# The forget gate's product moves to the front of the kernel, onto quarters of TensorE's columns, and the input's turnings get a third place in PSUM

## What is computed

```python
h = rmsnorm(x, norm_mix_g)
z = h @ w_in
u_pool = z[..., 0:512]; u_ssm = z[..., 512:1024]
q = z[..., 1024:1536]; k = z[..., 1536:2048]; v = z[..., 2048:2560]
logf = jax.nn.log_sigmoid(z[..., 2560:2568] + b_f)      # forget gate, 8 heads
```

## Time and profile before

| | |
|---|---|
| median of 3 runs | 1797.89 us (1792.35, 1797.89, 1801.83) |
| the profiled execution's own time | 1798.66 us |
| its span in the profile | 1796.9 us |
| TensorE (PE) busy | 1742.5 us, 97% |
| VectorE (DVE) busy | 1282.7 us, 71% |
| ScalarE (ACT) busy | 643.7 us, 36% |
| GpSimd (POOL) busy | 671.4 us, 37% |

### The profile page before, as it was taken

How to read it: one execution, slowest core, us unless ns; L and a number is a source line. 1 busy time by engine, 2 the same in 40 slices (tenths; PEclk the granted TensorE clock), 3 DMA queues, 4 the chain that set the end, 5 groups by cost and what they waited for, 6 DMA issues and landing times.

```text
span 1796.9 us, 31281 instructions
## 1 busy us (share of the span) xinstructions
PE 1742.5 (97%) x12261; PEld 1699.6 (95%) x12261; DVE 1282.7 (71%) x2006; ACT 643.7 (36%) x1239; POOL 671.4 (37%) x472
## 2 busy tenths in 40 slices
PE   7999999999998999999999988999999999999997
PEld 7999999999988989999999988999999999999997
DVE  6788662888886566554465489877777777699685
ACT  4210113566652222141002335444444444434343
POOL 4554434333354666422233223555554454000000
PEclk9999999999999999999999999999999999999999
DMA  8744838766734544365636331232222221998252
GB/s 267 220 129 137 268 108 246 194 175 176 183 111 146 129 106 94 88 191 208 196 109 207 98 108 37 74 91 89 73 73 73 73 73 55 343 345 283 93 192 90
DMA packets 265748, 267.25 MB, mean 149 GB/s; under 512 B 61985, under 2 KB 218637, under 8 KB 265154
## 3 DMA queue, kind: packets, MB, share of 16 engines
q1 hardware_dynamic: 251474, 234.04, 43.9%
q10 hardware_dynamic: 14128, 31.21, 5.0%
HBM read 181.37 MB, written 79.36 MB: 145 GB/s over the span
## 4 chain that ended last, share of the span: by engine, by line
PE 55%; DVE 6%; issue 3%; DMA 2%; ACT 1%; POOL 1%; SPq 0%; POOLq 0%; ACTq 0%; DVEq 0%
PE bank L156 51%; DMA act_raw<-act_scratch 1%; PE bank L2003 1%; PE bank L2013 1%; PE bank L2015 1%; DMA gate<-gate_scratch 1%; DVE merged L2300 1%; DVE x_forms L3087 0%; DVE prod L2293 0%; PE bank L2014 0%; DVE conv L3167 0%; DVE xt L3057 0%; POOL up_forms L2651 0%; DMA down_raw<-in_w_down 0%; PE bank L1988 0%
## 5 line engine op out<-in xcount | busy, mean ns | idle before, releaser
L156 PE MATMUL bank<-act_hi,w_hi 128*128 128x364 f32 (+1 forms) x1296 | 435.6, 336 | 2.5 <-PEq L86 1.6
L156 PE MATMUL bank<-act_lo,w_hi 128*128 128x364 f32 (+1 forms) x1296 | 427.1, 330 | 0.0
L156 PE MATMUL bank<-act_hi,w_lo 128*128 128x364 f32 (+1 forms) x1296 | 426.5, 329 | 0.0
L156 PE MATMUL bank<-x_forms,up_forms 128*128 128x272 f32 x1848 | 258.4, 289 | 3.6 <-DVE part_v L3135 2.0
L156 PEld LDWEIGHTS bank<-act_hi,w_hi 128*128 128x128 f32 x1296 | 244.9, 189 | 8.4 <-issue 4.3
L156 PEld LDWEIGHTS bank<-x_forms,up_forms 128*128 128x128 f32 x1848 | 242.2, 188 | 4.7 <-DVE up_forms L3119 2.3
L156 PEld LDWEIGHTS bank<-act_lo,w_hi 128*128 128x128 f32 x1296 | 244.8, 189 | 0.2
L156 PEld LDWEIGHTS bank<-act_hi,w_lo 128*128 128x128 f32 x1296 | 244.5, 189 | 0.0
L156 PE MATMUL bank<-act_form,down_form 128*128 128x272 f32 x1848 | 233.6, 288 | 3.6 <-DVE y_t L3243 1.8
L156 PEld LDWEIGHTS bank<-act_form,down_form 128*128 128x128 f32 x1848 | 231.7, 188 | 4.7 <-DVE y_t L3243 2.4
L2651 POOL TENSOR_TENSOR up_forms<-up_w_raw,up_forms 128x512 fp32r<-128x512 f32 x60 | 88.1, 1469 | 190.8 <-ACT up_forms L2866 190.8
(11 more groups left out here) (358 smaller groups left out, 3099.5 us busy)
## 6 DMA issues: line engine op xcount, KB each, us to landing
down_raw<-in_w_down SPq DMA_DIRECT2D x121, 256.0 KB, 4.3
w_raw<-in_w_in SPq DMA_DIRECT2D x44, 512.0 KB, 5.0
up_w_raw<-in_w_up SPq DMA_DIRECT2D x44, 512.0 KB, 4.9
gate<-gate_scratch ACTq DMA_DIRECT2D x24, 544.0 KB, 3.9
act_scratch<-ffn_act SPq DMA_DIRECT2D x22, 544.0 KB
act_raw<-act_scratch SPq DMA_DIRECT2D x44, 272.0 KB, 4.7
gate_scratch<-gate_out ACTq DMA_DIRECT2D x48, 182.0 KB, 2.7
w_raw<-in_w_out SPq DMA_DIRECT2D x14, 512.0 KB, 4.2
```

Source lines behind the costliest of these rows:

```text
L156: mm = pe.matmul(out, w(k), x(k)[:, c0:c0 + cn], start=first and k == ks[0] and n == 0, stop=last and k == ks[-1] and n == 2, skip_group_c ...
```

## The change

- The job "f" is gone from `JOBS`, and with it the split of the forget columns and DVE's six instructions that added the parts.
- `wf` is loaded by SP behind the fourth block of the input, and scaled on POOL before its second weight tile.
- Its product is taken in plain float32 from `xr`, the unrounded turned input. Each block of 128 frames is a moving operand of its own, and four blocks stand at four quarters of the array's columns (`tile_position=(0, 32 * q)`), so that their outputs lie at partitions 0, 32, 64 and 96 of one bank. `forget` is called for blocks 0 to 3 after the seventh turning, and for 4 to 7 and 8 behind the second group of q0.
- ACT copies the five pieces to a new tile `f_raw`; DVE multiplies it by `inv_b` in one instruction, right after k0 is emptied.
- The turnings have three places in PSUM instead of two; block j waits for the block that had its place before (`FREED`).
- ACT, not DVE, rounds blocks 3 and 6 into `m.hh`.
- The last bank of `acc[1]` holds the gate's sums; so q1's groups run in the order 0, 2, 1, and the third bank of `spread` is another one. A filler keeps the other tiles' addresses.

```diff
-JOBS = [("q", 0), ("q", 1), ("q", 2), ("q", 3), ("k", 0), ("f", 0), ("k", 1), ("k", 2), ("k", 3), ("v", 0), ("v", 1), ("v", 2),
+JOBS = [("q", 0), ("q", 1), ("q", 2), ("q", 3), ("k", 0), ("k", 1), ("k", 2), ("k", 3), ("v", 0), ("v", 1), ("v", 2),
-        by_k = [tr[:].rearrange("p b (k c) -> p (b k) c", c=P),
-                acc[1][:, 0:2].rearrange("p b (k c) -> p (b k) c", c=P)]
-        spread = [tr[:, 0], tr[:, 1], acc[1][:, 2]]
+        SLOT, FREED, ROUNDED = (0, 1, 2, 0, 1, 2, 0, 1, 0), (0, 0, 0, 1, 2, 3, 4, 5, 7), (3, 6)
+        by_slot = [x.rearrange("p b (k c) -> p (b k) c", c=P) for x in (tr[:], acc[1][:, 0:2], acc[0][:, 1:3])]
+        by_k = [by_slot[a] for a in SLOT]
+        spread = [tr[:, 0], tr[:, 1], acc[1][:, 1]]
+        f_bank = acc[1][:, 2]
...
+            sp.dma_start(wf[:], column_blocks(io["w_in"][0, :, 5 * W:5 * W + HEADS], KD)).then_inc(wf_ld, 16)
             for j in range(4, 9):
                 sp.wait_ge(x_turned, j - 3)
...
                 if t == 1:
+                    pool.wait_ge(wf_ld, 16)
+                    pool.tensor_tensor(wf[:], wf[:], m.gain1[:].unsqueeze(2).to_broadcast([P, KD, HEADS]), ALU.mult
+                                       ).then_inc(wf_scaled, 1)
                     pool.wait_ge(x_lo, 8)
...
-                if j >= 2:
-                    pe.wait_ge(x_lo, j - 1)
+                if j >= 3:
+                    pe.wait_ge(x_lo, FREED[j])
...
+            def forget(tokens):
+                pe.wait_ge(x_out, tokens[-1] + 1)
+                for k in range(KD):
+                    for j in tokens:
+                        (c0, cn), r0, at = TOK[j], 32 * (j % 4), j // 4 * P
+                        mm = pe.matmul(f_bank[r0:r0 + HEADS, at:at + cn], wf[:, k], xr[:, k, c0:c0 + cn], start=k == 0,
+                                       stop=k == KD - 1, tile_position=(0, r0))
+                mm.then_inc(f_mm, 1)
...
                 turn_x(5 + q)
+                if q == 1:
+                    pe.wait_ge(wf_scaled, 1)
+                    forget((0, 1, 2, 3))
             pe.wait_ge(x_lo, 6)
             group(0, 0, 1)
+            forget((4, 5, 6, 7))
+            forget((8,))
...
-            group(1, 1, 1)
+            pe.wait_ge(f_raw_done, 1)
+            group(1, 1, 2)
             pe.wait_ge(inv_done, 3)
-            group(1, 1, 2).then_inc(tile_mm, 1)
+            group(1, 1, 1).then_inc(tile_mm, 1)
...
+                if j in ROUNDED:
+                    act.activation(m.hh[:, :, c0:c0 + cn], by_k[j][:, :, 0:cn], ACT.Copy).then_inc(x_hi_act, 1)
...
+            act.wait_ge(f_mm, 3)
+            for q in range(4):
+                act.activation(f_raw[:, 0:TP].rearrange("h (a q c) -> h a q c", a=2, c=P)[:, :, q],
+                               f_bank[32 * q:32 * q + HEADS, 0:2 * P].rearrange("h (a c) -> h a c", c=P), ACT.Copy)
+            act.activation(f_raw[:, TP:T], f_bank[0:HEADS, 2 * P:2 * P + TS], ACT.Copy).then_inc(f_raw_done, 1)
...
-            slot(5)
-            dve.wait_ge(evac, 6)
+            dve.wait_ge(f_raw_done, 1)
+            dve.wait_ge(cache_st, 64)
+            dve.tensor_tensor(fq[:, 0:T], f_raw[:], m.inv_b[0:HEADS], ALU.mult).then_inc(f_part, 1)
+            dve.wait_ge(f_part, 1)
             dve.wait_ge(bf_ld, 16)
...
             tables.vector_turns(dve, (1, 2))
-            slot(6)
+            slot(5)
             low(("k", 1))
```

More of the change, by code:

```diff
@@ L905, in by_channel @@
     return gain.unsqueeze(2).to_broadcast([P, KD, P])
-JOBS = [("q", 0), ("q", 1), ("q", 2), ("q", 3), ("k", 0), ("f", 0), ("k", 1), ("k", 2), ("k", 3), ("v", 0), ("v", 1), ("v", 2),
+JOBS = [("q", 0), ("q", 1), ("q", 2), ("q", 3), ("k", 0), ("k", 1), ("k", 2), ("k", 3), ("v", 0), ("v", 1), ("v", 2),
         ("v", 3), ("u", 0), ("u", 1), ("m", 0), ("u", 2), ("m", 1), ("u", 3), ("m", 2), ("s", 0), ("s", 1), ("m", 3), ("s", 2),
         ("s", 3)]
-TILES = [job for job in JOBS if job[0] not in "fm"]
+TILES = [job for job in JOBS if job[0] != "m"]
 FIRST_TILE = {"u": 0, "s": MW, "q": 2 * MW, "k": 3 * MW, "v": 4 * MW}
@@ L1105, in sync @@
             for i, job in enumerate(JOBS):
-                if job[0] not in "fm" and 4 <= tile_of[job] + 2 < len(TILES):
+                if job[0] != "m" and 4 <= tile_of[job] + 2 < len(TILES):
                     load_w(tile_of[job] + 2)
@@ L1261, in tensor @@
                     pass
-                elif kind == "f":
-                    pe.wait_ge(wf_lo, 1)
-                    for g, (c0, cn) in enumerate(GROUPS):
-                        out = acc[a][0:FLO + HEADS, g, 0:cn]
-                        for k in range(KD):
-                            if k == 0:
-                                pe.matmul(out, wfhl[:, k], m.hh[:, k, c0:c0 + cn], start=True, stop=False)
-                            pe.matmul(out[0:HEADS], wfh[:, k], m.hl[:, k, c0:c0 + cn], start=False, stop=False)
-                            if k:
-                                mm = pe.matmul(out, wfhl[:, k], m.hh[:, k, c0:c0 + cn], start=False, stop=k == KD - 1)
-                    mm.then_inc(f_mm, 1)
                 elif kind == "m":
@@ L1377, in scalar @@
             high(("q", 1))
-            act.wait_ge(wf_scaled, 1)
-            act.activation(wfh, wf[:], ACT.Copy).then_inc(wf_hi, 1)
             high(("q", 2))
@@ L1443, in vector @@
             for j, (c0, cn) in enumerate(TOK):
-                x, hi = by_k[j % 2][:, :, 0:cn], m.hh[:, :, c0:c0 + cn]
-                dve.wait_ge(x_out, j + 1)
-                dve.tensor_copy(hi, x).then_inc(x_hi, 1)
-                dve.wait_ge(x_hi, j + 1)
+                x, hi = by_k[j][:, :, 0:cn], m.hh[:, :, c0:c0 + cn]
+                if j in ROUNDED:
+                    dve.wait_ge(x_hi_act, ROUNDED.index(j) + 1)
+                else:
+                    dve.wait_ge(x_out, j + 1)
+                    dve.tensor_copy(hi, x).then_inc(x_hi, 1)
+                    dve.wait_ge(x_hi, j + 1 - sum(r < j for r in ROUNDED))
                 dve.tensor_tensor(m.hl[:, :, c0:c0 + cn], x, hi.bitcast(F32), ALU.subtract).then_inc(x_lo, 1)
@@ L1459, in scaled @@
                 a = i % 2
[L1460 to L1472 removed]
+                dve.wait_ge(tile_mm, tile_of[JOBS[i]] + 1)
                 if kind == "u":
@@ L1648, in vector @@
             pooled_low(0)
-            scaled(14)
+            scaled(13)
             mix_low(0)
@@ L1712 @@
 GATES_ATT = 11
+F_RAW_AT = 214016
 EARLY = 4 * NB * (NTAB + C * SC + C * SC // 2)
```

70 lines of the change are left out of this document (24 added, 46 removed).

## The result

The changed kernel takes 1809.35 us in the median of 7 runs (1804.96 to 1810.39) against 1797.89: ratio 1.0064, 95% interval [1.0052, 1.0077], 11.5 us slower. The prediction was 1795.1 in a range to 1803, so it was wrong. The profiled execution took 1809.19 us, 10.5 us more than the one of before.

What follows compares the result with a forecast made beforehand. PE, busy nearly throughout, was taken as the bound. Front +4.9 - 3.5 + 0.9 = +2.3, job f -8.0 and wf's load -0.2 gave -5.9; waits behind POOL's squaring left -2.8: 1795.1 us in the median's terms, range 1788 to 1803.

Steps and rivals of the forecast that it cites:

- Job f, -8.0: PE around 88.68 to 96.63 us: removing the job's 48 matmuls saves 8.0 us.
- the product, +4.9: PE's front: the gate's product costs 4.9 us, two calls of 1.9 and one of about 1.1.
- the third place, -3.5: PE's front: a third place for turnings removes waits for DVE, 2.4 before the first group and 1.1 before the last turnings.
- The rival of serial quarters: Gate's product: quarters run one after another, calls cost 7.0 us each, the kernel ends slower at 1805.3; chance 0.06.
- The clock, +0.9 in the front: Front: if TensorE's pace still rises at about 19.5 us, the sixth turning falls before it, +0.9; bounds +0 and +1.5.
- the forecast's 41.8: End of the front: PE reaches the spread of the norms at 41.8 us, 2.3 later than before.
- wf's load, 0.2: Front: loading `wf` ahead of the fifth input block delays that block by 0 to 1.5 us, taken as 0.2.
- The last squaring at 105.0: POOL, tile 7: the last squaring, for which DVE waits, ends at 105.0 us; bounds 104.7 and 106.9.
- `vector_turns` takes 4.4 us: DVE behind the last squaring: it takes 4.4 us, as in the earlier trace, ahead of k1's emptying and k0's copies.
- the forecast 3.6: PE at about 107.8 us: a stall of 3.6 us at k0's turning, waiting for DVE's copy.
- Which I let through to the end, since what follows hangs on PE: Behind v0's emptying at 146.7 us: the gain of 2.8 us reaches the kernel's end unchanged.
- all cases together left 0.05: Whole kernel: chance 0.05 of ending slower by over 9 us, needing the serial quarters and more.

Runs made afterwards that it cites:

- seventh run: The change with the input's turnings back on two PSUM places, ACT still rounding two blocks: 1811.00 us, ratio 1.0075.
- eighth run: The change with the gate's product written block by block, so that no two quarters alternate: 1815.51 us, ratio 1.0099.
- fourth run: The kernel before with only the third place for the input's turnings, DVE still rounding all blocks and f still a job: 1798.46 us, ratio 0.9995.
- eleventh run: The kernel of the sixth run with the table's store on SP moved behind v2's and v3's stores: 1801.50 us, ratio 1.0021.
- fifth run: The kernel before with only the load of wf moved early, behind the input's fourth block: 1797.47 us, ratio 0.9998.
- third run: The change with POOL rounding tile 7 only when k1 is emptied, so not beside `vector_turns`: 1802.26 us, ratio 1.0023.
- The last run: The change with only 32 blanks (8x8 matmuls nobody reads, 128 instructions) added in PE's idle time of the front: 1802.21 us, ratio 1.0028.
- sixth run: The change with DVE's emptyings and turned-frame copies reordered ahead of pieces of the table, its later pieces put behind v0 to v3: 1804.31 us, ratio 1.0041.
- second: The change with DVE emptying k1 and copying k0's frames ahead of `vector_turns`, k2's emptying and k1's copies right behind: 1806.66 us, ratio 1.0045.

## Why the prediction was wrong

- **Job f, -8.0; the product, +4.9; the third place, -3.5.** Right for the first two: the calls take 1.93 and 2.81 us (3.0). The place with ACT's roundings is worth 3.7 at the spread (seventh run), of which the waits it removes are 2.4 and the rest is PE's pace. The rival of serial quarters is excluded for this order and shown real for the other (eighth run). The rule of the Trainium skill (TensorE: Matmul & The Clock Gate, Part 3, What overlaps and what doesn't) falls with it where the quarters alternate: 64 loads of 0.09 us standing alone would be 5.8 us, and the whole call takes 1.93. Not seen: alone the place is worth nothing at the end (fourth run).
- **The clock, +0.9 in the front.** 1.6 in the change's own profile and in the eleventh run's, nothing in six others; its bounds were 0 and 1.5. Without it the spread stood at 39.7, 2.1 us ahead of the forecast's 41.8. That the clock would also fall behind each wait, at 1.7 us a time, I had in no term: 5.1 us in this execution.
- **wf's load, 0.2.** No cost (fifth run).
- **The last squaring at 105.0.** 106.65, near the upper bound, since POOL's first squarings waited for DVE's three instructions of the gate (L354 1.28 us, L357 1.24). In the third run it was 105.2.
- **"`vector_turns` takes 4.4 us": the step that failed first.** I took it from the earlier trace rows, where POOL was idle, and gave it the same price with POOL's rounding of tile 7 behind the same squaring. It took 8.6; the third run, with nothing but POOL kept away, gives 4.3. With the squaring that makes 9.86 us of wait for the forecast 3.6.
- **"Which I let through to the end, since what follows hangs on PE": the step that failed next.** Behind 207 us another 6.2 are lost, 2.8 in longer waits at m1 and the attention and 3.4 in the clock behind them, and the prediction had nothing there. 191 more instructions on PE moved the loads of its instructions, and one fell on a store that the mixer waits for. The last run, in which 32 blanks move them away, takes both waits down to 0.76 and 0.92 without a halved clock and gives back 6.5 us by the ratios, 6.2 in the profiles, of which 1.9 are the front. That leaves 4.4 for these two waits and their clock. The way from load to store to wait is shown for m1; for the attention's wait only that the blanks changed it. The rest of the 11.5 is the wait at 107 with its clock, and the two aren't strictly a sum, as part of what one gives back the other would take. The table's store on SP is no part of it: in the change it was issued 5.0 us later than before (196.55 for 191.50), with PE.
- The rivals: none had this. The one that ended slower priced the wrong mechanism and had 0.06; all cases together left 0.05 for what happened.

## What to carry to other kernels

An instruction's time from a profile holds for the neighbours that it had there: when an edit moves POOL's large tiles beside DVE's small instructions, price the small ones at the length of the large. Before a saving on the busiest engine is let through to the end, follow back at each later stage the chain that ends just before its work, even where it hardly waits: at m0 of the kernel before PE waited for nothing and ACT 0.27 us for a store of v, and with PE 6 us early in the sixth run the same store cost PE 5.41. And a change of a few per mille in a nearly full kernel is compared with a blank control that has the same number of instructions.

## What the runs showed of the hardware

Blank matmuls change this kernel's time by some 6 us either way: +5.7 with 48 in the kernel before (1.8 of it the front), and about 6.5 less with 32 in the change. What they move is the queue of PE's instruction loads, packets of 16384 bytes that took 0.9 to 1.8 us and came every 20 us or so around 200 us; a 32 KB store beside one landed 1.3 to 1.9 us later. The Trainium skill (Runtime: NRT & Kernel Launch, Instruction fetch mechanics) says that the sequencer fetches its instructions by DMA in blocks of 256, at a cost that is mostly hidden. The traces agree with the block: 98 loads before, 99 with 191 instructions more, 100 with 384 more. It is hidden from PE, but not from whoever waits for the store beside it.

The granted clock was halved during or behind each of the 22 waits of PE of 2.69 us and more between 60 and 330 us in these kernels, and for 3.1 to 5.5 us of work; behind ten of the eighteen waits of 2.1 to 2.5 us (in the change yes, in the second and eighth run at m1 no), and behind one of 1.82. So a wait at m1 that grows from 0.94 to 2.18 us costs 1.2 or 2.9, and the wait's length alone doesn't decide which.
